# A decoder step with 32 experts on one core: 96-slot experts in plain f32 on four column quarters, and expert weights stored as contiguous half chunks

## What is computed

```python
logits = (t @ router_w) + router_b
top_v, top_e = lax.top_k(logits, TOP_K)          # TOP_K = 4 of 32
gate = softmax(top_v)
# for each expert e and each token sent to it:
#   up = x @ w_up[e] + b_up[e]                    (1024 -> 2048: a gate half and a linear half)
#   hidden = clamped SwiGLU(gate half, linear half)   (1024)
#   y += gate * (hidden @ w_down[e] + b_down[e])
```

## Time and profile before

| | |
|---|---|
| median of 3 runs | 1739.96 us (1731.2 to 1741.41) |
| span of the profiled execution | 1731.7 us |
| median less span | 8.3 us |
| TensorE busy | 1665.8 us, 96% |
| VectorE, ScalarE busy | 1137.0 us (66%), 888.9 us (51%) |
| expert weights | 384 loads of 1,024 KB |
| TensorE's granted clock | 0.990 on the mean |

### The profile page before, as it was taken

The page is one execution under the profiler, slowest core; times in us unless marked ns, Lnnn a source line. Parts: engine busy times, 40 slices in busy tenths (PEclk is TensorE's granted clock), DMA queues, the critical chain, the costliest instruction groups (busy, mean ns, idle before and its releaser), DMA issues.

```text
span 1731.7 us, 27748 instructions
## 1 busy us (share of the span) xinstructions
PE 1665.8 (96%) x10106; PEld 1295.3 (75%) x10106; DVE 1137.0 (66%) x1555; ACT 888.9 (51%) x1019; POOL 217.4 (13%) x260
## 2 busy tenths in 40 slices
PE   7999999999998999999999999999989999999998
PEld 4899988798777777767677686767768676776765
DVE  6866785655356868949385684939477593938661
ACT  5245655533423446647274664728375573727461
POOL 0022000003331033110001001001000101100100
PEclk9999999999999999999999999999999999999999
DMA  5063233114437329999999999999999999999996
GB/s 219 30 215 120 84 123 101 46 62 134 140 107 261 104 71 403 348 396 402 398 405 378 409 386 398 394 399 399 384 410 383 400 397 403 395 395 409 381 399 231
DMA packets 100436, 498.74 MB, mean 288 GB/s; under 512 B 16350, under 2 KB 33846, under 8 KB 49648
## 3 DMA queue, kind: packets, MB, share of 16 engines
q1 hardware_dynamic: 84288, 458.39, 67.3%
q0 software_dynamic: 15920, 38.71, 7.9%
q10 hardware_dynamic: 144, 0.55, 0.1%
HBM read 488.10 MB, written 25.35 MB: 297 GB/s over the span
## 4 chain that ended last, share of the span: by engine, by line
PE 73%; DMA 14%; DVE 7%; issue 3%; ACT 2%; POOL 0%; ACTq 0%; SPq 0%; DVEq 0%; POOLq 0%
DMA ring<-in_w_exp 13%; PE bank L1350 13%; PE bank L1367 12%; PE bank L1403 9%; PE bank L795 7%; PE bank L695 5%; PE bank L850 5%; PE bank L1418 4%; PE bank L722 3%; PE bank L1114 2%; DVE ring_rounded L2631 1%; PE bank L662 1%; PE bank L863 1%; PE bank L884 1%; PE bank L872 1%
## 5 line engine op out<-in xcount | busy, mean ns | idle before, releaser
L2631 DVE TENSOR_TENSOR ring_rounded<-ring,wide_rounded 128x2048 fp32r<-128x2048 f32 x126 | 283.7, 2285 | 21.5 <-ACT wide_rounded L1846 21.3
L1846 ACT ACTIVATE wide_rounded<-ring 128x2048 fp32r<-128x2048 f32 x126 | 236.6, 1912 | 86.4 <-DMA ring<-in_w_exp 72.6
L1350 PE MATMUL bank<-ring_rounded,slab_rounded 128*128 128x512 f32 x672 | 264.3, 394 | 0.0
L1350 PE MATMUL bank<-xn_rounded,slab_rounded 128*128 128x512 f32 x672 | 224.9, 407 | 1.2 <-DVE ring_rounded L2631 0.8
L2631 DVE TENSOR_TENSOR ring_rounded<-ring,xn_rounded 128x2048 fp32r<-128x2048 f32 x84 | 190.2, 2285 | 20.6 <-ACT xn_rounded L1846 19.2
L1367 PE MATMUL bank<-wide_rounded,slab_rounded 128*128 128x512 f32 x504 | 172.4, 403 | 9.3 <-DVE slab_rounded L2726 8.9
L1846 ACT ACTIVATE xn_rounded<-ring 128x2048 fp32r<-128x2048 f32 x84 | 159.5, 1909 | 22.8 <-DMA ring<-in_w_exp 19.3
L2772 DVE TENSOR_SCALAR slab<-bank 128x256 f32<-128x256 f32 x22 | 9.3, 424 | 237.6 <-PE bank L1403 237.6
L1350 PE MATMUL bank<-wide_rounded,slab_rounded 128*128 128x512 f32 x504 | 159.0, 390 | 0.0
L1403 PE MATMUL bank<-ring,slab 128*64 128x256 f32 x1408 | 156.2, 380 | 0.0
L1350 PEld LDWEIGHTS bank<-xn_rounded,slab_rounded 128*128 128x128 f32 x672 | 130.0, 193 | 33.5 <-ACT xn_rounded L1846 3.4
(11 more groups left out here) (553 smaller groups left out, 2988.2 us busy)
## 6 DMA issues: line engine op xcount, KB each, us to landing
ring<-in_w_exp SPq DMA_DIRECT2D x384, 1024.0 KB, 14.0
ring<-in_w_blk SPq DMA_DIRECT2D x40, 512.0 KB, 3.3
slab<-in_w_tok SPq DMA_DIRECT2D x4, 1304.0 KB, 15.0
ring<-in_w SPq DMA_DIRECT2D x8, 512.0 KB, 3.3
ring<-in_w_out SPq DMA_DIRECT2D x2, 2048.0 KB, 15.5
xn<-in_xT SPq DMA_DIRECT2D x4, 520.0 KB, 7.9
ring<-in_k_cmp SPq DMA_DIRECT2D x32, 64.0 KB, 3.5
ring<-in_k_cmp POOLq DMA_DIRECT2D x32, 64.0 KB, 2.6
```

Of the source, the lines that this page charges most:

```text
L1350: r = mm(bank[:, c, :], a[:, 4 * h + k, :], w[:, k, :], start=False, stop=h == 1 and i == 11)
L1846: fn(WH[(2 * c + h) % 6], ring[:, half_of(c, h)], ACT.Copy).then_inc(S["wh_ready"], 1)
L2631: v.tensor_tensor(ring_r[:, half_of(c, h)], ring[:, half_of(c, h)], WHf[(2 * c + h) % 6], ALU.subtract)\
```

## The change

The caps of the 32 places become a table: 96 slots for 20 places, 64 for 11, 128 for one. All experts are multiplied in plain f32, straight from the ring; the rounding on ScalarE, the remainder on VectorE, the buffers `WH` and all rounded row buffers go.

A 96-slot expert uses the array in four quarters of 32 columns. Quarters 0 to 2 take 32 token rows each and the first 384 columns of the chunk; quarter 3 takes the last 128 columns for all 96 rows, as three products of 128 columns (`product`). For each block of 128 channels there are thus six products. The 64-slot experts keep their two halves, now for `w_down` as well; the one 128-slot expert has one product of 512 columns. The gates of the moved rows need extra columns (`moved_gates`) and extra scaling instructions.

`w_down` is cut by output columns, like `w_up`, and its pieces are used in the order (4,0), (5,0), (4,1), (5,1) (`PIECE_ORDER`). Every piece has a semaphore of its own. In DRAM each half chunk is now 1 MB in one run (128 rows of 8 KB). The tokens' rows are turned before the first down product of the expert instead of in the middle. At the start three small loads for the moved gates of experts 0 and 1 are added on GpSimd's queue.

```diff
-FEW = 64
-TRIPLES = 9
+FEW, MID = 64, 96
+GROUP = (MID, FEW, MID, MID, FEW, MID)
+BEFORE, BEHIND = 2, 2
+WIDE_AT = 2 + len(GROUP) * BEFORE
+LAST = (MID, FEW, MID, FEW, FEW)
+CAP = (MID, MID) + GROUP * BEFORE + (P,) + GROUP * BEHIND + LAST
...
             def expert_half(e, c, h):
-                sp.dma_start(ring[:, half_of(c, h)], d["w_exp"][bass.ds((e * 6 + c) * P, P), h * HALF:(h + 1) * HALF])\
-                    .then_inc(ring_in[eslot[c]], 16)
+                sp.dma_start(ring[:, half_of(c, h)], d["w_exp"][bass.ds((e * 12 + (2 * c + h)) * P, P), :])\
+                    .then_inc(piece_in[2 * c + h], 16)
...
+            def product(c, slots, rows, w, first, last):
+                if slots == P:
+                    return mm(bank[:, c, :], rows(0, P), w, start=first, stop=last)
+                if slots == FEW:
+                    for y in range(2):
+                        r = mm(bank[64 * y:64 * y + 64, c, 0:256], rows(0, 64), w[:, 256 * y:256 * y + 256], start=first, stop=last)
+                    return r
+                for g in range(3):
+                    mm(bank[32 * g:32 * g + 32, c, 0:384], rows(32 * g, 32), w[:, 0:384], start=first, stop=last)
+                for g in range(3):
+                    r = mm(bank[96:128, c, P * g:P * (g + 1)], rows(32 * g, 32), w[:, 384:512],
+                           start=first and g == 0, stop=last and g == 2)
+                return r
...
+            def up_half(n, c, h, slots):
+                pe.wait_ge(piece_in[2 * c + h], 16 * n + 32)
+                w = weights(c, h)
+                for k in range(4):
+                    r = product(c, slots, lambda a, m: XT[:, 4 * h + k, a:a + m], w[:, k, :], False, h + k == 4)
+                r.then_inc(S["half_used"], 1)
...
+            def down(n, slots, meanwhile=None):
+                turn_hidden(n, slots, 0)
+                if meanwhile is not None:
+                    meanwhile()
+                pe.wait_ge(S["y_scaled"], n + 1)
+                pe.wait_ge(S["hh_ready"], 2 * n + 1)
+                down_half(n, 4, 0, slots)
+                turn_hidden(n, slots, 1)
+                down_half(n, 5, 0, slots)
+                pe.wait_ge(S["hh_ready"], 2 * n + 2)
+                down_half(n, 4, 1, slots)
+                down_half(n, 5, 1, slots)
...
-            def low_half(b, c, h):
-                dve.wait_ge(S["wh_ready"], 12 * b + 2 * c + h + 1)
-                v.tensor_tensor(ring_r[:, half_of(c, h)], ring[:, half_of(c, h)], WHf[(2 * c + h) % 6], ALU.subtract)\
-                    .then_inc(S["wl_ready"], 1)
...
             gather(GX[1][0:CAP[1], :], rows_of(1))
+            for g in range(3):
+                dma(moved_gates[96:128, 0:2, g:g + 1], by_expert[32 * g:32 * g + 32, 0:2, 1:2].bitcast(F32),
+                    allow_slow_non_contiguous=True).then_inc(S["ent_in"], 16)
```

More of the change, by code:

```diff
@@ L1332, in up_chunk, with down_half, up_first @@
+            def down_half(n, c, h, slots):
+                pe.wait_ge(piece_in[2 * c + h], 16 * n + 16)
+                w = weights(c, h)
+                for k in range(4):
+                    r = product(c, slots, turned_hidden(slots, h, k), w[:, k, :], h + k == 0, h + k == 4)
+                r.then_inc(S["half_used"], 1)
+            def up_first():
+                pe.wait_ge(S["pick_set"], 1)
+                pe.wait_ge(S["xt_ready"], 1)
+                for c in range(4):
                     if c >= 2:
@@ L1968, in triple @@
[L1968 to L1977 removed]
+                fn(XT[:, :, 0:slots], bank[:, 6:8, :].rearrange("p b (k t) -> p (b k) t", k=4)[:, :, 0:slots], ACT.Copy)\
+                    .then_inc(S["xt_ready"], 1)
@@ new lines, in block_of, with groups @@
+            def block_of(n, b, slots, following, by_column=True):
+                gated(n, slots, 0)
+                gated(n, slots, 1)
+                hidden_copied(n, slots, 0)
+                if following:
+                    turned_rows(n + 1, following)
+                hidden_copied(n, slots, 1)
+                scaled(n, b, slots, by_column)
+            def groups(count, first, following):
+                with act.Fori(0, count) as t:
+                    for i, slots in enumerate(GROUP):
+                        block_of(len(GROUP) * t + (first + i), (first + i) % 2, slots, (GROUP + (following,))[i + 1])
@@ L1986, in _ @@
             act.wait_ge(y0_out[2], 16)
-            block_of(0, 0, "all")
-            block_of(1, 1, "few")
-            with act.Fori(0, TRIPLES) as t:
-                triple(t)
-            pair()
-            few_block(NE - 1, last=True)
+            block_of(0, 0, CAP[0], CAP[1])
+            block_of(1, 1, CAP[1], GROUP[0])
+            groups(BEFORE, 2, P)
+            block_of(WIDE_AT, WIDE_AT % 2, P, GROUP[0])
+            groups(BEHIND, WIDE_AT + 1, GROUP[0])
+            for n in range(LAST_AT, NE):
+                block_of(n, n % 2, CAP[n], CAP[n + 1] if n + 1 < NE else None)
             act.wait_ge(S["ovf_ready"], 2)
@@ L2801, in _, with groups @@
+            def groups(count, first):
+                with dve.Fori(0, count) as t:
+                    for i, slots in enumerate(GROUP):
+                        block_of(len(GROUP) * t + (first + i), (first + i) % 2, slots, True)
             pick_expert(0, pick_two)
@@ L3024, in _constants @@
     e = np.arange(NE)
-    few = np.isin(e, SMALL_AT)
+    cap = np.array(CAP)
     bias = e - np.where(e == 0, 40000, 0) - np.where(e == 1, 20000, 0)
     ranks = np.zeros(NE)
-    ranks[[0, 1] + list(SMALL_AT) + [n for n in e if n >= 2 and not few[n]]] = e
+    ranks[[0, 1] + sorted(range(2, NE), key=CAP.__getitem__)] = e
     rank_in = np.zeros((P, 160), f)
-    rank_in[:, 0:32], rank_in[:, 32:64], rank_in[:, 64:96], rank_in[:, 96:128] = bias, ranks, np.where(few, P - FEW, 0), SLOTS * e
+    rank_in[:, 0:32], rank_in[:, 32:64], rank_in[:, 64:96], rank_in[:, 96:128] = bias, ranks, P - cap, SLOTS * e
     row = np.arange(P)
```

550 lines of the change are left out of this document (164 added, 386 removed).

## The result

| kernel | median us | runs | span of the profiled execution |
|---|---|---|---|
| before | 1736.55 | 4 (1731.2 to 1741.41) | 1731.7 |
| changed | 1746.99 | 4 (1745.34 to 1748.11) | 1743.6 |

The ratio is 1.0068, 95% interval 1.0041 to 1.0095. I forecast 1,700 us with 1,672 to 1,765 as the range: the time lies inside the range, but the gain of 2.3% did not come; the kernel is 0.7% slower. That the range holds the time is no merit of the forecast's mechanism: its upper end stood for the memory at its old rate.

A forecast was written before the change was run, and what follows sets the result against it. Partly TensorE (big experts), partly memory (behind the small one) bound the kernel, 33.1 us an expert. Memory then bounds: last product 1,682, plus 7.6 and 2, span 1,692, plus 8.3 is 1,700 us (1,672 to 1,765).

The forecast's parts named there:

- Memory: Weight stream in the expert loop: 31.9 us an expert at 422 GB/s with token rows; 31 experts 989 us, to 1663.
- the share does not separate the windows while the rate does: Expert loop: 419 to 422 GB/s after the small expert, 379 in the first big one, DMA share 1.00 in both.
- The 23.84 us of transfer: Behind the small expert the chain is a ring transfer for 23.84 us: TensorE used up pieces faster than they come.
- the memory was the bound already: Expert stage: 33.1 us an expert is all the memory gives; about 1,735 us, no change; chance 0.12.
- the signs of being wrong: Block above 0.72 us; TensorE-only chain, rate below 390, packets beside issue waits; slices at 395, landing waits in every expert.
- Instructions: TensorE's 1,228 records per 96-slot expert taken at nothing; as rival, 2.24 us a packet, 1,899 us, chance 0.08.
- The unit: TensorE's time for one 128-channel block of a 96-slot expert, its six products side by side: 0.66 us.
- Its own end: TensorE alone as the bound, its sum of 995 us from 671 on, would end at 1,684 us.
- Layout: Contiguous half chunks in DRAM: nothing gained; as rival 433 for 422 GB/s, about 1,688 us, chance 0.03.
- ScalarE and VectorE: Roundings (22.9 us) and remainders (27.4 us) leave each big expert; their going was costed at nothing, having had cover.
- The moved gates: Three added loads on GpSimd's queue at the start cost 0 to 6 us; with extra transposes, 6 us on block 0.
- The 8.3 us from span to median: Added after the forecast span of 1,692 us to reach the 1,700 us median; might be as small as 0.

The follow-up runs named there:

- written out: The changed kernel with TensorE's loops over the groups unrolled, so that TensorE takes no jump between groups: 1746.97 us, 1.0087 of the kernel before.

## Why the prediction was wrong

**The step that failed is the one headed "Memory"**, and before it the sentence that the share does not separate the windows while the rate does. I took 422 GB/s, from seven slices on a plateau, as what the memory gives over the whole stage, and the 379 of the first window as a loss due to TensorE. Removing two thirds of the big experts' products won 3 us. What mostly differs between the windows is who else moves data: where token rows come and go, the rate falls to 340 GB/s and less, and the plateaus are for the most part the time between two experts' token rows.

The prediction's reading was not wrong in everything. From 1003 to 1012 us no token row moves in the kernel before and the rate is 381 GB/s all the same, and without any token rows it still dips once a turn. TensorE's pace does show in the rate. But what it takes there is not what the time consists of: with that work gone the mean rate from 800 to 1600 us is the same (304.52 for 304.71 MB). How it is made up for, no run shows. The 23.84 us of transfer in the earlier trace rows also say less than I read in them. They run from a piece's issue to its landing, and TensorE is not idle in them: 9.94 of 10 us in the second window of the earlier trace rows. The second big expert takes 40.6 us (from its first bias product at 1065.35 to the next expert's at 1105.93) where the first took 35.4, so late landings cost some 5 us a turn there.

The term, sized again: 31 experts of 31.9 us were 989 us. Measured in the kernel before it is 31 x 33.03 = 1,024, so 35 us were missing, nearly the forecast's whole gain of 40. In the changed kernel it is 31 x 33.47 = 1,038, 49 us more than forecast, where the whole miss is 47. Of the 1.1 us an expert that were missing, about 0.3 is the weights' rate (30.1 for 29.8) and the rest the token rows, 2.9 to 3.2 instead of 2.0. The numbers for it stood in the earlier trace rows: the slices' mean was at hand, and 33.1 us an expert was in the same part of the prediction, as the measured period. A sum that lands below a measured period because of a better rate needs a reason why the average was not already that rate.

**The rival that came true** is "the memory was the bound already", at 0.12; its 1,735 us missed what follows. I held against it that the swing of the rate follows TensorE's pace. It follows GpSimd's transfers more. Of the signs of being wrong, the slices that stay near 395 came; the waits for landings came only in part, 34 of them and 37.6 us in all, because TensorE's own work is nearly as long as the transfers'.

**Instructions** had a right sign and a wrong path, and the forecast put them at nothing for the wrong reason. I priced them through TensorE's stalls, 2.24 us a packet or nothing. The one stall that gave this price was misread as well: it stands from 546.4 to 548.7 us, behind the window of the earlier trace rows, and the transfers were nearly idle in it, not saturated (share 0.07):

```profile
546.40:548.70 2.30, 0.06 (x6) 0.01 (x3) 2.26 (x2) 0.00 (x0) 0.00 (x0) 1.00 0.07 29
```

TensorE did stop at jumps, for 5.4 us, as the page "Runtime: NRT & Kernel Launch" of the Trainium skill says under instruction fetch mechanics for a branch out of the store; the trace agrees. The 2 us in the sum for the loops' branches were thus too few, but the stalls did not reach the end (written out: 1746.97). What cost was the fetching itself, 108 packets more on engines that had no time: at their bare occupancy 7 us, at the 0.14 to 0.20 us of the two estimates 15 to 22 us, beside 12 to 18 us measured by the ratios. "Packets are few beside the 384 MB" was the wrong comparison: by bytes the 108 packets are less than two of the weights' 384 pieces, but by the time that they hold an engine they are more, 1.07 us for 16 KB where two weight packets take 0.65.

**TensorE's terms held.** The unit: 0.66 forecast, 0.655 measured. A 96-slot expert: 34.5 forecast, 34.2 measured. Its own end: 1,684 forecast, 1,692 without token rows. The rule of the Trainium skill on packing small matmuls ("TensorE: Matmul & The Clock Gate", Part 3), by which the unit would have been an estimated 0.83, does not hold for these quarters: with 384 columns in three and 128 in the fourth a block takes 0.655.

**The small terms.** Layout at nothing: right, by a run in either direction. ScalarE and VectorE at nothing: nothing speaks against it, since TensorE's waits for VectorE were late landings. The moved gates: of the 6 us on block 0 one wait of 1.1 us is left for them and one of 2.1 us for gathered rows. The 8.3 us from span to median were mostly the scatter of three runs: every run is some 1.7 us longer than its own span, and after the change the median is 3.4 us above the profiled span.

## What to carry to other kernels

Before taking work from an engine, divide the bytes of a whole stage by its time, and take no plateau of a better rate as available before you know why the average is lower: look at what else moves data outside the plateau. Busy shares do not decide it. TensorE looked 96% busy and had no say; the shares of all queues added up to 101% where the transfers were the bound, and to 100% in the kernel without token rows, where TensorE was. One run with two thirds of the suspected engine's work left out decides it. On a full set of transfer engines everything small has a price above its bytes, token rows and TensorE's own code too. Here token rows cost 48 to 55 us with all arithmetic in place and 99 us with half of it, while two thirds of the big experts' arithmetic were worth 3 us.

## What the runs showed of the hardware

- Four column quarters with unlike lengths (384, 384, 384 and three times 128) overlap fully: 0.655 us a block, against 0.647 that three plain products of 384 columns alone need by the earlier trace rows, an estimate.
- 4 KB token rows beside 8 KB weight packets: 6.8% of the engines' time from 690 us on, 72 us (some 4,350 packets of 265 ns), and up to 99 us of the kernel's. Gathers (54 us) and additions (45 us) cost nearly alike.
- A packet of TensorE's instructions (16 KB) holds one of 16 transfer engines for 1.07 us. While the transfers are full, the runs put its price at 0.07 to 0.20 us of the kernel's time; 0.067 is its bare occupancy.
- A busy share of the transfer engines near 1.00 goes with 401 GB/s where TensorE is the bound and with 419 GB/s where it is not, both without token rows. It does not tell a full set of engines from one that is held back.
- A jump back over a body of some 5,800 records costs TensorE 5.2 to 5.4 us; here a ring of 12 pieces covered most or all of it.
- No version that was run and does the whole work beats the kernel before; half chunks in it are the same within 0.2%.
